# Computing the sample's memory readout already transposed in the mLSTM cell of a streaming encoder step

## The reference

```python
inter = b + m[..., None]
m_t = jnp.maximum(inter, jnp.max(dlog, axis=-1))
w = jnp.exp(dlog - m_t[..., None])
s_inter = jnp.exp(inter - m_t)
qk = jnp.einsum('bthd,bshd->bhts', qc, kc) * w
num = s_inter[..., None] * jnp.einsum('bthd,bhde->bhte', qc, cm) + jnp.einsum('bhts,bshe->bhte', qk, vc)
den = s_inter * jnp.einsum('bthd,bhd->bht', qc, nv) + jnp.sum(qk, axis=-1)
h = num / jnp.maximum(jnp.abs(den), jnp.exp(-m_t))[..., None]
```

## Time and profile before

| what | value |
|---|---|
| median of 3 runs | 2336.69 us (2334.42 to 2340.99) |
| the profiled execution's own time | 2340.99 us |
| its span | 2339.2 us |
| PE busy | 2197.7 us, 94% of the span |
| PE weight loads busy | 2045.1 us, 87% |
| DVE busy | 1271.7 us, 54% |
| POOL busy | 1222.1 us, 52% |
| ACT busy | 363.7 us, 16% |
| mean granted TensorE clock | 0.972 of full speed |

### The profile page before, as it was taken

One profiled execution on the slowest core, in us unless ns is written; L12 is line 12 of the kernel. 1 busy time (PEld: TensorE's weight loads), 2 busy tenths in 40 slices (PEclk: granted clock), 3 DMA queues, 4 the chain that ended last, 5 costly groups with the idle time before them and its releaser, 6 DMA issues.

```text
span 2339.2 us, 38876 instructions
## 1 busy us (share of the span) xinstructions
PE 2197.7 (94%) x15775; PEld 2045.1 (87%) x15775; DVE 1271.7 (54%) x2185; ACT 363.7 (16%) x659; POOL 1222.1 (52%) x1185
## 2 busy tenths in 40 slices
PE   7978888999999999999999998999889999999997
PEld 7977777997999999999999995577589799999996
DVE  6798896432553452657566644672644245345263
ACT  4211212112200000021012022431311220000001
POOL 5546677642655656576666650032145165656562
PEclk8998999999999999999999999999999899999998
DMA  5212324320222221223344333442231022222221
GB/s 188 81 65 73 136 91 158 145 73 19 74 89 81 82 90 72 90 88 129 134 151 154 133 108 118 191 183 90 113 127 64 28 73 89 74 90 72 90 83 48
DMA packets 38185, 235.83 MB, mean 101 GB/s; under 512 B 4512, under 2 KB 7584, under 8 KB 12712
## 3 DMA queue, kind: packets, MB, share of 16 engines
q1 hardware_dynamic: 21600, 154.15, 18.7%
q10 hardware_dynamic: 16456, 79.80, 8.9%
HBM read 200.05 MB, written 33.89 MB: 100 GB/s over the span
## 4 chain that ended last, share of the span: by engine, by line
PE 76%; DVE 19%; issue 2%; ACT 2%; POOL 1%; DMA 0%; ACTq 0%; DVEq 0%; POOLq 0%
PE psum L508 62%; PE psum L538 12%; PE psum L524 1%; DVE hl L1923 1%; DVE hh L1919 1%; DVE tm L1616 1%; DVE xc L1988 1%; DVE CA L1629 1%; DVE xnl L1448 1%; POOL wlo L460 1%; DVE hr L1912 0%; DVE hs L1915 0%; DVE ss L1433 0%; DVE xnl L2157 0%; DVE C L2214 0%
## 5 line engine op out<-in xcount | busy, mean ns | idle before, releaser
L458 POOL TENSOR_SCALAR whi<-raw 128x512 fp32r<-128x512 f32 x584 | 424.0, 726 | 1028.9 <-PE psum L508 996.2
L460 POOL TENSOR_TENSOR wlo<-raw,whi 128x512 fp32r<-128x512 f32 x584 | 802.4, 1374 | 48.7
L508 PE MATMUL psum<-xnh,whi 128*128 128x288 f32 (+1 forms) x2816 | 622.7, 299 | 43.0 <-DVE xnl L1448 17.8
L508 PE MATMUL psum<-xnl,whi 128*128 128x288 f32 (+1 forms) x2816 | 617.0, 297 | 0.0
L508 PE MATMUL psum<-xnh,wlo 128*128 128x288 f32 (+1 forms) x2816 | 616.5, 297 | 0.0
L508 PEld LDWEIGHTS psum<-xnh,whi 128*128 128x128 f32 x2816 | 463.8, 192 | 52.8 <-issue 40.6
L508 PEld LDWEIGHTS psum<-xnl,whi 128*128 128x128 f32 x2816 | 463.8, 191 | 0.0
L508 PEld LDWEIGHTS psum<-xnh,wlo 128*128 128x128 f32 x2816 | 463.7, 191 | 0.0
L508 PE MATMUL psum<-hh,whi 128*128 128x288 f32 x1024 | 219.3, 295 | 2.1 <-DVE hl L1923 2.1
L508 PE MATMUL psum<-hl,whi 128*128 128x288 f32 x1024 | 218.5, 294 | 0.0
L508 PE MATMUL psum<-hh,wlo 128*128 128x288 f32 x1024 | 217.9, 294 | 0.0
(11 more groups left out here) (405 smaller groups left out, 2657.7 us busy)
## 6 DMA issues: line engine op xcount, KB each, us to landing
raw<-in_w SPq DMA_DIRECT2D x146, 1024.0 KB, 4.7
C<-in_C ACTq DMA_DIRECT2D x4, 1024.0 KB, 5.2
o_cp<-mvt ACTq DMA_DIRECT2D x4, 1024.0 KB, 3.9
o_cs<-C ACTq DMA_DIRECT2D x4, 1024.0 KB, 4.8
t_xc<-xc ACTq DMA_DIRECT2D x3, 1152.0 KB, 6.8
t_z<-mv ACTq DMA_DIRECT2D x3, 1152.0 KB, 4.2
t_q<-mq ACTq DMA_DIRECT2D x3, 1152.0 KB, 4.2
t_k<-mk ACTq DMA_DIRECT2D x3, 1152.0 KB, 4.2
```

The costliest lines, as they stand in the source:

```text
L458: pool.tensor_scalar(whi[:, s, c], raw[:, s, c], 1.0, 1.0, ALU.mult, ALU.mult).then_inc(S("slab_hi"), 1)
L460: ins = pool.tensor_tensor(wlo[:, s, c], raw[:, s, c], whi[:, s, c].bitcast(F32), ALU.subtract)
L508: ins = pe.matmul(bank(g, 2 * m + b)[:, 0:t1 - t0], W[wi][:, kk, m0 + m, :], r[:, kk, t0:t1], start=(at_first and wi == 0 and r is rh), st ...
```

## The change

The numerator of the sample is computed with features on the partitions from the start. For each tile e of 128 features, four matmuls have a 128 x 128 block of C0 as the stationary operand and the 64 columns of `qs` moving, and a fifth has 128 columns of `vt5` (64 partitions) as the stationary operand and `wts` moving. They write bank 2, 64 columns a tile, at the end of the group. The transposes, the copy to `tm` on ACT and the two semaphores between PE and ACT are gone, and ACT reads bank 2 where it read bank 3. The arithmetic is the same.

```diff
                 pe.wait_ge(S("cell_c"), 16 * (n + 1))
-                for d in range(ML_T):
-                    mm(B[2][0:TS, :], qs[:, d, :], C0[:, d, :], d == 0, False)
-                mm(B[2][0:TS, :], wts[:], vt5[:], False, True).then_inc(S("smp_num"), 1)
                 for j in range(NTB):
                     mm(B[0][:, P * j:TP], ones[:], wt[:, blk(j):blk(j) + TP - P * j], j == 0, j == NTB - 1)
                 for d in range(ML_T):
                     mm(B[1][:, 0:TS], n0b[:, d, :], qs[:, d, :], d == 0, False)
                 mm(B[1][:, 0:TS], ones[0:TS, :], wts[:], False, True)
-                pe.wait_ge(S("smp_rows"), n + 1)
                 for e in range(ML_T):
-                    ins = pe.transpose(B[3][:, TS * e:TS * e + TS], tm[0:TS, 1, P * e:P * e + P], ident[0:TS, 0:TS])
+                    o = B[2][:, TS * e:TS * e + TS]
+                    for d in range(ML_T):
+                        mm(o, C0[:, d, P * e:P * e + P], qs[:, d, :], d == 0, False)
+                    ins = mm(o, vt5[:, P * e:P * e + P], wts[:], False, True)
                 group_close(ins, g)
...
                 ch.mark(ins, free[g % 2], S("cell_kt"))
-                act.wait_ge(S("smp_num"), n + 1)
-                act.activation(tm[0:TS, 1, 0:ML_DH], bank(GR["cell", h, "den"], 2)[0:TS, :], ACT.Copy).then_inc(S("smp_rows"), 1)
                 if n:
...
-                ch.mark(act.activation(qs[:].rearrange("p e t -> p (e t)"), bank(g, 3)[:, 0:ML_T * TS], ACT.Copy),
+                ch.mark(act.activation(qs[:].rearrange("p e t -> p (e t)"), bank(g, 2)[:, 0:ML_T * TS], ACT.Copy),
                         free[g % 2], S("cell_abs"))
```

## The result

The changed kernel takes 2356.32 us in the median of six runs (2354.53 to 2358.49), the kernel before 2339.06 us in six (2334.42 to 2340.99): ratio 1.0077, interval 1.0063 to 1.0090, some 17 to 18 us slower. On another chip the ratio was 1.0064 (1.0049 to 1.0079). The forecast was +0.85 us; the interval excludes it. The ratios leave out one slow execution of the kernel before, of 7571.74 us, in the group that e11_between_wide and after_again are compared with.

A forecast was written before the change was run, and what follows sets the result against it. PE was taken to bound the cell loop. Its +0.35 us a head, less slack, summed as 0.35 + 0.01 + 0.14 + 0.35 = +0.85 us, giving 2336.69 + 0.85 = 2337.5 us, range 2333 to 2342.

The forecast's parts named there:

- What bounds the kernel: Cell loop: PE is three quarters of the chain; den groups of first and fourth heads fully on it, two have slack.
- the second head's slack: Before kv in the second head, 0.34 us is waiting for ACT, so +0.35 us on PE adds only +0.01 there.
- The removed work, 4.89 us a head: den group on PE: 4.55 us of C,qs and vt,wts matmuls plus 0.34 us of transposes go.
- The round trip to ACT was covered and its removal worth zero: ACT's four copies of 0.59 us go; PE never waited late for them; at most 1 us in the first head.
- The added tile at 1.29 us: den group: each five-matmul tile takes 3 x 0.220 + 0.27 + 0.36 us; four tiles 5.16 us, +0.35 us a head on PE.
- The granted clock stays at 1.00: Through all four den groups the clock was expected at 1.00, so added matmuls cost only their pitch.
- rival 3: Short matmuls lower the clock in every head, 3.4 us each, +14.4 us in all, 2351.1 us; chance 0.04.
- Rival 2, bare weight loads: den group: 128-partition loads uncovered at 0.18 us a record, +2.39 us a head, +9.0 us in all, 2345.7 us; chance 0.03.

The follow-up runs named there:

- e11_between_wide: Changed kernel with fours of 128-partition matmuls behind the four column sums, 64-partition ones together at the end, 128 columns streamed; 2343.09 us, ratio 1.0003 to the kernel before.
- after_again: The changed kernel itself, run again on the same chip and in the same hour as e11_between_wide; 2356.19 us, ratio 1.0064 to the kernel before.
- e4_keep_copy: Changed kernel with a 64 x 512 copy kept on ACT in the old place, result unread, no wait for PE; 2359.98 us, ratio 1.0079 to the kernel before.
- e6_tiles_between: Changed kernel's same instructions reordered, one tile of five short matmuls behind each of the four column sums; 2345.84 us, ratio 1.0034 to the kernel before.
- e7: Kernel before with the changed form in the first and fourth heads alone, old form in second and third; 2348.84 us, ratio 1.0047.
- e10: Kernel before, all old work kept, with the changed kernel's twenty short matmuls added behind the gates, result unused; 2374.49 us, ratio 1.0146.
- e2: Changed kernel with the twenty matmuls streaming 128 columns instead of 64 (the same 64 twice), same order; 2347.45 us, ratio 1.0026 to the kernel before.
- e9: e1 with 32 columns streamed instead of 64, readout of the sample's second 32 tokens left out; 2352.53 us, ratio 1.0059 to the kernel before.
- e1: Changed kernel with the den group reordered: all 16 matmuls over 128 partitions first, then the four over 64; 2344.14 us, ratio 1.0017 to the kernel before.
- e3: Changed kernel with 16 matmuls over 128 partitions, then four over 64, all streaming 128 columns instead of 64; 2341.06 us, ratio 1.0002 to the kernel before.
- e8: Changed kernel with 128-partition matmuls in fours behind the column sums, then gates, then all 64-partition matmuls together; 2340.42 us, ratio 1.0007 to the kernel before.
- e5: Changed kernel with the twenty short matmuls moved to the head of the den group, before the column sums; 2353.84 us, ratio 1.0070 to the kernel before.

## Why the prediction was wrong

- *What bounds the kernel*: right. The loss arrived through PE in the stretches named, and the second head's slack was used up.
- *The removed work, 4.89 us a head*: right as a term. *The round trip to ACT was covered and its removal worth zero*: right as far as it can be told. e4_keep_copy shows no difference from the copy, to within some 6 us; that PE did not wait for it is read from the rows of before.
- *The added tile at 1.29 us*: mis-sized, 1.40 us. I put "0.27 + 0.36 us for four records" as the whole price of there and back. In rows 4 the matmuls that follow the step back are 128 columns wide and of another group, so what the first load after the return costs was not in that sum. Eight records take 1.04 us after a switch where the gates took 0.93. Four tiles are 4 x 0.11 = 0.44 us more, wt,ones 0.03 less: +0.75 us a head instead of +0.35. Through the slacks that is 0.75 + 0.41 + 0.54 + 0.75 = 2.5 us, against the 0.85 forecast, and the loop of e6_tiles_between, at full clock, is 251.37 − 248.84 = 2.53 us longer than before. This alone would have left the time within 0.3%.
- *The granted clock stays at 1.00*: this is the step that failed. It was rival 3, "if streams of short matmuls brought that on in every head", with a chance of 0.04 and +14.4 us. The loop grew by 18.5 us, 2.5 of them pitch; 16 are the clock, by the difference from the loop of e6, which has the same matmuls in another order at full clock (12.8 in the profile of after_again). So the price in the rival, 3.4 us a head, was near; what I had wrong was that it would not happen. That the new form causes the fall is shown by e7 (it falls in the changed heads alone) and e10 (it falls with the old work still there). All runs fit a cause in the thin stream, few columns over a stretch of time; the alternation alone does not bring the clock down. This is shown by e2 (twice the columns, same alternation, 1.00), e9 (half the columns, little alternation, it falls) and e6 (same instructions, spread between long ones, 1.00). The alternation has a part in it all the same: at 64 columns and without it (e1) the clock stays at 1.00 from `den` to `kvs`. It stretches a tile from 1.10 to 1.40 us and so thins the stream further; whether it acts in any other way on the clock was not tried.
- The argument that I used against it, "48 short records of transposes and scores before the second `den` group kept the clock at 1.00, and the new stage leaves PE no gap", had two faults. The old group began with ten long records right behind those 48, while the new one follows them with 2.2 us of long and 6.9 us of short ones. And I took a gap to be what brings the clock down. The Trainium skill, TensorE: Matmul & The Clock Gate, section Why this matters for your kernels, also speaks of idle gaps between bursts as what lowers the clock. The trace does not agree that a gap is needed: here PE was busy 10.10 of 10.10 us and 11.60 of 11.60 us and the clock fell to 0.89 and 0.76.
- *Rival 2, bare weight loads*: not seen; the records over 128 partitions come every 0.11 us in the tiles too. The rule that I cited, from section The mechanism of the same page of the Trainium skill, lets a load overlap only when it goes to another row group; the section also names a background weight buffer as a second way, which I left out. The trace does not agree with the rule as I used it: inside a tile the loads over the same 128 partitions start some 0.06 us ahead of their own matmuls, while others run. It is the load behind a change of the partition count that is late: it starts together with its own matmul (both at 1492.73 in the second head).

What stays open. The falls at about 1471 and 1530 us in the changed kernel, in the `score` groups, stand behind a pause of 1.8 us that the kernel before has as well, without a fall. e1, e3, e8 and e11 have the first of them, e2 and e6 neither, and the second profile of the changed kernel, after_again, has neither. So one kernel can have them or not; each profile is a single execution, and no experiment was aimed at it. They account for 3.4 us or less. In e6 the pitch explains 2.5 of the 5 to 11 us, and its clock in the loop is at full. Its profiled span is 4.2 us over that of the kernel before: 2.5 in the loop, 3.0 ahead of it, where the code is the same, and 1.4 less behind it. What the rest of the ratio is stays open, and so does what in the stream of short matmuls the clock answers to, and where the limit lies.

## What to carry to other kernels

Turning a product around to get its result in the wanted layout can trade few long matmuls for many short ones at nearly the same PE time (9.11 us against 8.36 here), and lose far more than the difference, since whatever PE does while the clock is down runs at half speed: the long matmuls behind the thin stretch in the changed kernel, the thin stretch itself in e5. Where short matmuls are needed, put them between long ones, keep those with the same number of partitions together, and look at the granted clock of the stretch behind them before counting records. A removed round trip between engines is worth only what someone was waiting for.

## What the runs showed of the hardware

- The granted clock can fall with PE busy without a pause. In and behind the twenty matmuls with 64 moving columns that alternate between 128 and 64 partitions it was 0.74 to 0.89 (first head of the changed kernel). It was 1.00 with 128 columns at nearly the same pitch (e2, 1.50 us a tile against 1.40), 1.00 with 64 columns and the partition counts grouped (e1), 1.00 with the tiles put between longer matmuls (e6), and 0.83 to 0.96 with 32 columns, grouped (e9, `den` and `num` of the first two heads).
- 64 more moving columns are almost free under a 128-column f32 weight load: 32 records take 3.77 us with 128 columns (e3_grouped_wide), 3.71 with 64 (e1_grouped) and 3.69 with 32 (e9_narrow, third head).
- A change between 128 and 64 partitions and back costs about 0.3 us (a tile takes 1.40 us, ten records at 0.11 would be 1.10). In the trace the first weight load after a change starts together with its own matmul, the others in the tile some 0.06 us ahead of theirs.
- The runs of e9_narrow spread over 13 us (2344.72 to 2357.94), and two profiles of the changed kernel have falls of the clock in different places, with loops of 267.37 and 264.18 us; a single run says little here.
